# A hybrid encoder layer in float32: TensorE's four loops written out as straight code

## The chip, the cores and the metric

The kernel runs on one core of a Trainium2 chip. The metric is the device time of one launch in microseconds (us); lower is better. Of the kernel before there are three timed runs, 1295.16, 1296.4 and 1301.4 us, with the median at 1296.4 us. Beside them one execution was recorded by the hardware profiler, and every duration below comes from that one execution, whose span is 1296.8 us.

The core's engines are TensorE (PE in the profile; its weight loads are listed apart as PEld), VectorE (DVE), ScalarE (ACT), GpSimd (POOL) and SyncE (SP). Each engine has a sequencer that reads its own program, and engines meet only at semaphores. A name with a q behind it (PEldq, DVEq) is an engine's sequencer in the trace.

## What is computed

One mixer layer over 272 positions (16 learned meta tokens and 256 inputs) of width 2048, then a final norm:

```python
xn = rmsnorm(h, norm_g)
z = xn @ w_in                                   # 2048 x 16384: all branches, gates and merge gates
hy_in, hy_gate, fn_in, fn_gate, qkv, na_gate, merge = jnp.split(z, idx, axis=-1)
hy_in = short_conv(hy_in, conv_w, conv_b)
u, x1, x2 = jnp.split(hy_in, HY_ORDER + 1, axis=-1)
kf = hyena_filters(L, w1, b1, w2, b2, w3, b3, w4, freq, decay)
y_a = hyena_mixer(u, x1, x2, kf, skip) * jax.nn.silu(hy_gate)
y_b = fourier_mixer(fn_in) * jax.nn.silu(fn_gate)
y_c = neighborhood_attention(q, k, v, rpb, meta_bias) * jax.nn.silu(na_gate)
g_a, g_b, g_c = jnp.split(jax.nn.sigmoid(merge), N_BRANCH, axis=-1)
m = g_a * (y_a @ w_a) + g_b * (y_b @ w_b) + g_c * (y_c @ w_c)
return h + m @ w_out
```

## The kernel before

**Products.** Every large product is made of three float32r matmuls on high and low parts (`three`, L529 to L532: high x high, low x high, high x low). The weights are cut into slabs of 1024 x 256 elements, 1 MB each. SP streams a slab into one of four buffers `raw`; ACT rounds it into `w_hi` (L835), DVE makes `w_lo` from the rest (L1101), and PE runs 48 matmuls over it (`proj_slab`, 2 column halves x 8 k-steps x 3). `w_hi` and `w_lo` have two places each. The semaphores are `w_landed`, `hi_done`, `lo_done` and `slab_used`: SP reloads a buffer when the slab four before is split, ACT splits slab n when PE has used slab n - 2.

**Stages of PE's program.** After a small filter network and the transposition of x come four stages, each held in a hardware loop or around one:

- filters (L607): the spectra of the long convolutions, per chunk of 256 channels. The loop runs once over two chunks, two more chunks follow as straight code.
- chunks (L704): four passes `c`, one for each chunk of channels. A pass has 20 slabs (10 blocks of columns, `BLOCKS`, of two slabs each), and between the slabs the work of the three mixers on that chunk: transposes, the transforms `forward` and `inverse`, `scores`, `turn_p`, `attend`, `fnet_channels`, `fnet_tokens`. A pass ends with `fnet_tokens` (L667 and around; its last matmuls are those of L535).
- merge (L776): four passes `i` of 18 slabs each.
- output (L804): four passes of 4 slabs each.

Inside a loop the pass number is a register, so a wait such as `pe.wait_ge(proj_read, c * NBLK + (t // 2 + 1))` (L707) compares a semaphore with a register that is computed at its place.

**The other engines.** DVE, ACT and SP have loops of their own over the same passes (DVE L1283, L1389, L1407; ACT L1001, L1064, L1085; SP L349, L355, L361), and POOL loops over passes 1 to 3 of the chunks (L490). POOL's loop stores the branch results (`store_y`, L482), loads the attention bias of the next chunk as eight transfers and two more (`load_bias`, L457 and L460), adds the mask to it (L467), and then loads that chunk's first filter spectrum (`load_spectrum`, L471 and L473) into `kspec`. DVE reads `kspec` at slab t = 4 of a pass (`spectra`, L1249 to L1252), and PE waits for what DVE made of it at t = 5 (`y_full`).

**Order at the edge of a chunk pass.** The first slab of a pass is split by ACT and DVE during t = 18 of the pass before, the second during t = 19. PE's waits at t = 0 are for the evacuation of the block but one before (`proj_read`) and for the slab's low part (`lo_done`). DVE still has the last gate (L1230 to L1232) and the product with it (L1348) to do when PE comes to the edge.

Of the kernel before, what the change touches and what calls it, by code (L numbers as in the profile page):

```python
# [40 lines left out]
CH = C // CC  # L41
# [18 lines left out]
JB = D // CC  # L60
# [63 lines left out]
def build(nc, x, meta, w_stream, tables, zT, negt_in, mask_in, ident_in, params_in, mlp_in, w1, w2, w3, w4,  # L124
# [116 lines left out]
    with ExitStack() as ctx:  # L241
# [284 lines left out]
        def _(pe):  # L526
# [36 lines left out]
            def make_h4(c, j, par):  # L563

                p, n = TOK[FORDER[j]]
                if j == 0:
                    pe.wait_ge(w4_landed[par], (c - par) * 8 + 16)
                pe.wait_ge(h4_read, c * 3 + (j + 1))
                for o_ in range(2):
                    last = mm(ps[0:n, 6 + o_, :], hid[:, p:p + n], w4s[:, par, o_, :, :].rearrange("p d n -> p (d n)"),  # L570
                              start=True, stop=True)
                last.then_inc(h4_mm, 1)
# [22 lines left out]
            def filters(c, par, more):  # L595

                for j in range(3):
                    add_spectra(c, j, (0, 1, 2))
                    if j == 0:
                        make_h4(c, 2, par)  # L600
                    elif more:
                        make_h4(c + 1, j - 1, 1 - par)
                    add_spectra(c, j, (3, 4, 5))

            make_h4(0, 0, 0)
            make_h4(0, 1, 0)
            with pe.Fori(0, CH // 2 - 1) as cc:  # L607
                filters(cc * 2, 0, True)
                filters(cc * 2 + 1, 1, True)
            filters(CH - 2, 0, True)  # L610
# [11 lines left out]
            def turn(src, bank):  # L622

                for t, (p, n) in enumerate(TOK):
                    for i in range(2):
                        dst = ps[:, bank, CC * t + 128 * i:CC * t + 128 * i + 128] if t < 2 else \
                            ps[0:n, bank + 1, 128 * i:128 * i + 128]
                        last = nc.tensor.transpose(dst, src[:, i, p:p + n], ident[:, :])  # L628
                last.then_inc(t_mm, 1)
# [71 lines left out]


            pe.wait_ge(k_evac, CH * 6 + 2)
            with pe.Fori(0, CH) as c:  # L704
                for t in range(S1):
                    name, _, n = BLOCKS[t // 2]
                    if t % 2 == 0:  # L707
                        pe.wait_ge(proj_read, c * NBLK + (t // 2 + 1))
                    if t == 2:
                        pe.wait_ge(k_evac, CH * 6 + 4)  # L710
                    pe.wait_ge(lo_done, c * S1 + (NCONST + t + 1))
                    proj_slab(t % 2, 2 * (t // 2 % 2), t % 2, L - n)
                    if t == 3:
                        pe.wait_ge(proj_read, c * NBLK + 3)
                        pe.wait_ge(k_evac, CH * 6 + 6)
                        turn(u, 4)
                    if t == 4:
                        pe.wait_ge(t_lo, c * 3 + 1)
                        forward(0, 4)
                        forward(1, 5)  # L720
                    if t == 5:
                        pe.wait_ge(y_full, c * 6 + 1)
                        forward(2, 4)
                    if t == 6:
                        pe.wait_ge(proj_read, c * NBLK + 5)
                        scores(0)
                    if t == 8:
                        pe.wait_ge(p_done, c * HC + 1)
                        turn_p()
                        pe.wait_ge(proj_read, c * NBLK + 6)  # L730
                        pe.wait_ge(y_full, c * 6 + 3)
                        turn(v, 4)
                    if t == 9:
                        pe.wait_ge(pt_lo, c * HC + 1)
                        scores(1)
                        pe.wait_ge(t_lo, c * 3 + 2)
                        pe.wait_ge(ylo_done, c * 6 + 3)
                        inverse(0)
                    if t in (10, 12, 14):
                        hh = (t - 8) // 2  # L740
                        pe.wait_ge(p_done, c * HC + hh + 1)
                        attend(hh - 1)
                        turn_p()
                    if t in (11, 13):
                        hh = (t - 7) // 2
                        pe.wait_ge(o_done, c * HC + hh - 1)
                        scores(hh)
                    if t == 11:
                        pe.wait_ge(z_done, c + 1)
                        turn(x1, 4)  # L750
                    if t == 12:
                        pe.wait_ge(t_lo, c * 3 + 3)
                        forward(0, 4)
                        forward(1, 5)
                    if t == 13:
                        pe.wait_ge(y_full, c * 6 + 4)
                        forward(2, 4)
                    if t == 15:
                        pe.wait_ge(ylo_done, c * 6 + 6)
                        inverse(NM)  # L760
                        pe.wait_ge(o_done, c * HC + 3)
                        attend(3)
                    if t == 16:
                        pe.wait_ge(proj_read, c * NBLK + 10)
                        pe.wait_ge(ya_done, c + 1)
                        fnet_channels(0, 4)
                        fnet_channels(1, 5)
                    if t == 17:
                        pe.wait_ge(n1_lo, c * 3 + 1)
                        fnet_channels(2, 4)  # L770
                    if t == 19:
                        pe.wait_ge(n1_lo, c * 3 + 3)
                        fnet_tokens()


            with pe.Fori(0, JB // 2) as i:  # L776
                for t in range(S2):
                    b, part = t % 9 // 3, t % 3
                    m = t // 3
                    pair = 2 * ((2 * m + (part == 2)) % 4)  # L780
                    if part == 0:
                        pe.wait_ge(gate_done, i * 6 + (m + 1))
                        if m == 0:
                            pe.wait_ge(proj_read, NBLK * CH + 1)
                        if m == 1:
                            pe.wait_ge(yb_done, CH)
                    if part == 2:
                        pe.wait_ge(br_read, i * 6 + (m + 1))
                        if m == 0:
                            pe.wait_ge(proj_read, NBLK * CH + 2)  # L790
                        pe.wait_ge(blo_done, b + 1)
                    pe.wait_ge(lo_done, i * S2 + (NCONST + W2 + t + 1))
                    if part < 2:
                        proj_slab(t % 2, pair, part, NM)
                    else:
                        for nt in range(2):
                            for k in range(8):
                                last = three(ps[:, pair + nt, 0:NG], w_hi[:, t % 2, k, 128 * nt:128 * nt + 128],
                                             w_lo[:, t % 2, k, 128 * nt:128 * nt + 128], yb_hi[:, b, k, :], yb_lo[:, b, k, :],
                                             k == 0, k == 7)  # L800
                        last.then_inc(slab_used, 1)


            with pe.Fori(0, JB // 2) as i:  # L804
                for t in range(4):
                    half, nb = t // 2, t % 2
                    if half == 0:
                        pe.wait_ge(h_sum, i * 2 + (nb + 1))
                    if t == 0:
                        pe.wait_ge(gate_done, 3 * JB + 2)  # L810
                        pe.wait_ge(mlo_done, JB // 2)
                    if t == 1:
                        pe.wait_ge(br_read, 3 * JB + 2)
                    if t == 2:
                        pe.wait_ge(mlo_done, JB)
                    pe.wait_ge(lo_done, i * 4 + (NCONST + W3 + t + 1))
                    for tt in range(2):
                        for k in range(8):
                            kk = 8 * half + k
                            last = three(ps[:, 2 * nb + tt, 0:CC], m_hi[:, kk, 128 * tt:128 * tt + 128],  # L820
                                         m_lo[:, kk, 128 * tt:128 * tt + 128], w_hi[:, t % 2, k, :], w_lo[:, t % 2, k, :],
                                         kk == 0, kk == KT - 1)
                    last.then_inc(slab_used, 1)
# [675 lines left out]
```

## Time and profile before

| what | us |
|---|---|
| median of three timed runs | 1296.4 |
| lowest and highest of them | 1295.16, 1301.4 |
| span of the profiled execution | 1296.8 |
| PE busy in it | 1216.5 (94%) |
| DVE busy | 744.6 (57%) |
| ACT busy | 525.1 (40%) |
| POOL busy | 98.4 (8%) |

The page counts 22710 executed instructions over all engines.

Only PE is busy nearly all the time, so what matters is where PE is idle, for how long, and at which clock it works. In the profile a matmul's duration is longer than the distance to the next one's start, since matmuls overlap; distances between starts give the rate. The chunk passes begin at 123.4, 293.7, 456.4 and 618.8 us, the merge passes at 773.4, 879.7, 986.1 and 1090.8 us, the output at 1193.6 us; PE's last matmul starts at 1286.4 us.

### The profile page before, as it was taken

How to read it: one execution, taken by the hardware profiler on the slowest of the kernel's cores; microseconds unless marked ns; L12 is line 12 of the kernel's file. 1: busy time of each engine (PE TensorE's matmuls, PEld its weight loads, DVE VectorE, ACT ScalarE, POOL GpSimd, SP SyncE). 2: the span in 40 equal slices, each digit the busy share in tenths (PEclk: the TensorE clock that was granted, in tenths of full speed). 3: DMA queues.
4: the chain of work that ended last, by engine and by line, in shares of the span. 5: the costliest groups of instructions: out<-in, count | busy, mean ns of one | idle time of the engine just before them, and what ended most of it. 6: DMA issues, size and time to landing. Idle time of an engine off the chain costs nothing.

```text
span 1296.8 us, 22710 instructions
## 1 busy us (share of the span) xinstructions
PE 1216.5 (94%) x9454; PEld 1157.2 (89%) x9454; DVE 744.6 (57%) x842; ACT 525.1 (40%) x589; POOL 98.4 (8%) x130
## 2 busy tenths in 40 slices
PE   3898979989999899998999999999999999999996
PEld 1345979989999899998999999999999999999996
DVE  5675456873668736687366876544444444445454
ACT  5575334433344333443334435333333343343433
POOL 2130300022000220002200000000000000000000
PEclk9998989998999999999899999999999999999998
DMA  8144834256442564425543255454445454555652
GB/s 285 33 151 166 178 112 149 108 167 168 148 145 105 168 171 150 148 106 163 171 148 138 90 215 212 182 196 164 182 178 178 180 194 166 192 185 212 252 169 91
DMA packets 33396, 211.28 MB, mean 163 GB/s; under 512 B 4567, under 2 KB 4792, under 8 KB 10248
## 3 DMA queue, kind: packets, MB, share of 16 engines
q1 hardware_dynamic: 25976, 184.80, 40.2%
q0 software_dynamic: 7328, 25.04, 7.8%
q8 instruction: 83, 1.36, 0.4%
q14 instruction: 9, 0.07, 0.0%
HBM read 200.13 MB, written 9.70 MB: 162 GB/s over the span
## 4 chain that ended last, share of the span: by engine, by line
PE 76%; DVE 11%; issue 6%; ACT 4%; DMA 2%; POOL 1%; SPq 0%; ACTq 0%; DVEq 0%; POOLq 0%
PE ps L530 25%; PE ps L532 24%; PE ps L531 24%; ACT w_hi L835 3%; DVE gexp L1231 2%; DVE w_lo L1101 2%; PE ps L570 1%; DMA xin<-x 1%; PE ps L556 1%; DVE hm L1180 1%; DVE prod L1249 1%; DVE sd L1184 1%; DVE sd L1183 1%; DVE prod L1250 1%; PE ps L628 1%
## 5 line engine op out<-in xcount | busy, mean ns | idle before, releaser
L1101 DVE TENSOR_TENSOR w_lo<-raw,w_hi 128x2048 fp32r<-128x2048 f32 x168 | 385.5, 2295 | 426.5 <-ACT w_hi L835 426.5
L530 PE MATMUL ps<-xn_hi,w_hi 128*128 128x256 f32 (+2 forms) x2048 | 586.5, 286 | 28.9 <-issue 28.9
L531 PE MATMUL ps<-xn_lo,w_hi 128*128 128x256 f32 (+2 forms) x2048 | 584.7, 285 | 0.0
L532 PE MATMUL ps<-xn_hi,w_lo 128*128 128x256 f32 (+2 forms) x2048 | 584.5, 285 | 0.0
L835 ACT ACTIVATE w_hi<-raw 128x2048 fp32r<-128x2048 f32 x166 | 317.6, 1913 | 528.5 <-PE ps L532 528.2
L530 PEld LDWEIGHTS ps<-xn_hi,w_hi 128*128 128x128 f32 x2048 | 390.7, 191 | 31.6 <-issue 30.1
L532 PEld LDWEIGHTS ps<-xn_hi,w_lo 128*128 128x128 f32 x2048 | 390.7, 191 | 0.0
L531 PEld LDWEIGHTS ps<-xn_lo,w_hi 128*128 128x128 f32 x2048 | 389.5, 190 | 0.0
L530 PE MATMUL ps<-yb_hi,w_hi 128*128 128x256 f32 x384 | 108.8, 283 | 1.1 <-DVE yb_lo L1101 1.1
L532 PE MATMUL ps<-yb_hi,w_lo 128*128 128x256 f32 x384 | 108.6, 283 | 0.0
L531 PE MATMUL ps<-yb_lo,w_hi 128*128 128x256 f32 x384 | 108.6, 283 | 0.0
L530 PEld LDWEIGHTS ps<-yb_hi,w_hi 128*128 128x128 f32 x384 | 73.6, 192 | 1.3 <-issue 1.3
L531 PEld LDWEIGHTS ps<-yb_lo,w_hi 128*128 128x128 f32 x384 | 73.6, 192 | 0.0
L532 PEld LDWEIGHTS ps<-yb_hi,w_lo 128*128 128x128 f32 x384 | 73.6, 192 | 0.0
L530 PE MATMUL ps<-w_hi,m_hi 128*128 128x256 f32 x256 | 72.5, 283 | 0.5 <-DVE w_lo L1101 0.5
L531 PE MATMUL ps<-w_lo,m_hi 128*128 128x256 f32 x256 | 72.4, 283 | 0.0
L532 PE MATMUL ps<-w_hi,m_lo 128*128 128x256 f32 x256 | 72.4, 283 | 0.0
L990 ACT ACTIVATE y_hi<-prod 128x512 fp32r<-128x512 f32 (+1 forms) x24 | 15.2, 632 | 119.5 <-DVE prod L1252 119.5
L530 PEld LDWEIGHTS ps<-w_hi,m_hi 128*128 128x128 f32 x256 | 49.1, 192 | 0.8 <-DVE w_lo L1101 0.8
L531 PEld LDWEIGHTS ps<-w_lo,m_hi 128*128 128x128 f32 x256 | 49.1, 192 | 0.0
L532 PEld LDWEIGHTS ps<-w_hi,m_lo 128*128 128x128 f32 x256 | 49.1, 192 | 0.0
L1231 DVE RECIPROCAL gexp<-gexp 128x512 f32<-128x512 f32 x12 | 40.2, 3354 | 0.4
(239 smaller groups left out, 1304.8 us busy)
## 6 DMA issues: line engine op xcount, KB each, us to landing
raw<-w_stream SPq DMA_DIRECT2D x168, 1024.0 KB, 4.8
raw<-tables SPq DMA_DIRECT2D x4, 1024.0 KB, 20.2
kspec_grid<-kstage POOLq DMA_DIRECT2D x4, 1024.0 KB, 4.6
kspec<-kspec_grid POOLq DMA_DIRECT2D x8, 512.0 KB, 3.6
bias_t<-rpb POOLq DMA_DIRECT2D x32, 96.0 KB, 9.1
branch_y<-ystage POOLq DMA_DIRECT2D x12, 256.0 KB, 2.4
y_raw<-branch_y POOLq DMA_DIRECT2D x3, 1024.0 KB, 5.1
xin<-x SPq DMA_DIRECT2D x2, 1024.0 KB, 7.8
```

Of the source, the lines that this page charges most:

```text
L530: mm(out_ap, a_hi, b_hi, start=first, stop=False)
L531: mm(out_ap, a_hi, b_lo, start=False, stop=False)
L532: return mm(out_ap, a_lo, b_hi, start=False, stop=last)
L556: last = nc.tensor.transpose(ps[:, k % 4, p:p + n], xin[0:n, t, 128 * k:128 * k + 128], ident[0:n, 0:n])
L570: last = mm(ps[0:n, 6 + o_, :], hid[:, p:p + n], w4s[:, par, o_, :, :].rearrange("p d n -> p (d n)"), start=True, stop=True)
L628: last = nc.tensor.transpose(dst, src[:, i, p:p + n], ident[:, :])
L835: A(w_hi[:, par, :, :].rearrange("p k n -> p (k n)"), raw[:, slot, :], ACT.Copy).then_inc(hi_done, 1)
L990: ins = A(y_hi[0:n, f, :, :], prod[0:n, 2, :, :], ACT.Copy)
L1101: return V.tensor_tensor(dst, src, hi.bitcast(F32), ALU.subtract)
L1180: V.tensor_tensor(hm[0:n, :, :, :].rearrange("p o d n -> p o (d n)"), ps[0:n, 6:8, :], env.rearrange("p o d n -> p o (d n)"), ALU.mult).th ...
L1183: V.tensor_tensor(sd[0:n, 0, :, :], hm[0:n, :, 0, :], hm[0:n, :, 1, :], ALU.add)
L1231: link(V.reciprocal(gexp[:, :, :], gexp[:, :, :]))
```

## The change

Four lines: each `Fori` of PE becomes a Python loop, so PE's program has every pass written out, with constants in its waits.

```diff
-            with pe.Fori(0, CH // 2 - 1) as cc:
+            for cc in range(0, CH // 2 - 1):
                 filters(cc * 2, 0, True)
                 filters(cc * 2 + 1, 1, True)
...
-            with pe.Fori(0, CH) as c:
+            for c in range(CH):
                 for t in range(S1):
...
-            with pe.Fori(0, JB // 2) as i:
+            for i in range(JB // 2):
                 for t in range(S2):
...
-            with pe.Fori(0, JB // 2) as i:
+            for i in range(JB // 2):
                 for t in range(4):
```

The programs of DVE, ACT, POOL and SP are the same in both, loops included. PE's matmuls are the same and in the same order.

PE's program at the end of a chunk pass, before: behind the last matmuls of `fnet_tokens` stand the pass counter and the branch back to the loop's head (the head itself is shown next); `ISA` rows are waits against registers and register work.

```order
L531 MATMUL ps<-fsin_lo,y_hi 128x256
L532 MATMUL ps<-fsin_hi,y_lo 128x256
L535 MATMUL ps<-ftok_hi,y_hi 128x256
L535 MATMUL ps<-fsin_hi,y_hi 128x256
L704 REGISTER_ALU
L704 COMPARE_AND_BRANCH
L776 UNCONDITIONAL_BRANCH
```

The head of the chunk loop, before, behind the last matmul of the filters:

```order
L532 MATMUL ps<-sd_hi,filt_lo 16x512
L704 UNCONDITIONAL_BRANCH [waits k_evac]
L704 ISA
L711 ISA [waits proj_read]
L530 MATMUL ps<-xn_hi,w_hi 128x272 [waits lo_done]
```

The same place after the change, end of pass 0 and start of pass 1:

```order
L531 MATMUL ps<-fsin_lo,y_hi 128x256
L532 MATMUL ps<-fsin_hi,y_lo 128x256
L535 MATMUL ps<-ftok_hi,y_hi 128x256
L535 MATMUL ps<-fsin_hi,y_hi 128x256
L530 MATMUL ps<-xn_hi,w_hi 128x272 [waits lo_done,proj_read]
L531 MATMUL ps<-xn_lo,w_hi 128x272
```

The counter and the branch are gone, and the first matmul of the next pass follows the last of this one, with the same two semaphores waited for.

The end of a merge pass on PE, before, with what follows it when the loop is left:

```order
L530 MATMUL ps<-yb_hi,w_hi 128x256
L531 MATMUL ps<-yb_lo,w_hi 128x256
L532 MATMUL ps<-yb_hi,w_lo 128x256
L776 REGISTER_ALU
L776 COMPARE_AND_BRANCH
L804 UNCONDITIONAL_BRANCH
```

And after the change, between merge passes 0 and 1:

```order
L530 MATMUL ps<-yb_hi,w_hi 128x256
L531 MATMUL ps<-yb_lo,w_hi 128x256
L532 MATMUL ps<-yb_hi,w_lo 128x256
L530 MATMUL ps<-xn_hi,w_hi 128x256 [waits lo_done,proj_read,gate_done]
L531 MATMUL ps<-xn_lo,w_hi 128x256
```

Here too only the counter and the branch have gone from between two matmuls. PE's program has 2592 such rows before and 9333 after.

## Rows read from the trace of the kernel before

**Rows 1.** The page: busy time of PE, and its share of the span.

```profile
PE 1216.5 (94%) x9454; PEld 1157.2 (89%) x9454; DVE 744.6 (57%) x842; ACT 525.1 (40%) x589; POOL 98.4 (8%) x130
```

**Rows 2.** The page: the chain that ended last, by engine.

```profile
PE 76%; DVE 11%; issue 6%; ACT 4%; DMA 2%; POOL 1%; SPq 0%; ACTq 0%; DVEq 0%; POOLq 0%
```

**Rows 3.** Waits of PE: who waited for whom, total us, times, longest us.

```profile
PE ps L530 <- issue: 28.9, 6, 8.3
...
PE ps L530 <- DVE prod L1252: 7.7, 1, 7.7
```

**Rows 4.** Timeline of PE at pass edges: start us, us, what, [idle before].

```profile
286.05 0.28 PE L535 MATMUL ps<-fsin_hi,y_hi 80*128 80x256 f32 x1
293.68 0.59 PE L530 MATMUL ps<-xn_hi,w_hi 128*128 128x272 f32 x1 [7.34 <-issue]
...
456.42 0.59 PE L530 MATMUL ps<-xn_hi,w_hi 128*128 128x272 f32 x1 [7.66 <-issue]
...
618.83 0.59 PE L530 MATMUL ps<-xn_hi,w_hi 128*128 128x272 f32 x1 [8.30 <-issue]
...
879.65 0.58 PE L530 MATMUL ps<-xn_hi,w_hi 128*128 128x256 f32 x1 [2.00 <-issue]
```

**Rows 5.** PE's branches by loop line: ns min/median/max, first and last start.

```profile
L704 PEldq COMPARE_BRANCH  x4: 83/9381/10216, 284.2 to 771.4; - x4
...
L776 PEldq COMPARE_BRANCH  x4: 76/3654/3831, 875.5 to 1191.5; - x4
...
L804 PEldq COMPARE_BRANCH  x4: 76/215/228, 1215.4 to 1284.5; - x4
...
L607 PEldq COMPARE_BRANCH  x1: 93/93/93, 82.5 to 82.5; - x1
```

**Rows 6.** Windows, 5.6 us each: busy us (count), granted clock, DMA share, GB/s.

```profile
123.40:129.00 5.60, 5.60 (x46) 5.60 (x45) 0.00 (x0) 0.68 (x2) 1.26 (x2) 1.00 0.99 389
293.67:299.27 5.60, 5.59 (x24) 5.60 (x25) 0.00 (x0) 0.00 (x0) 0.00 (x0) 0.50 0.98 158
456.41:462.01 5.60, 5.59 (x32) 5.60 (x33) 0.00 (x0) 0.00 (x0) 0.00 (x0) 0.70 1.06 168
618.82:624.42 5.60, 5.59 (x27) 5.60 (x28) 0.00 (x0) 0.00 (x0) 0.00 (x0) 0.57 0.93 162
879.65:885.25 5.60, 5.60 (x34) 5.60 (x35) 4.27 (x4) 0.64 (x2) 0.00 (x0) 0.70 0.57 181
```

**Rows 7.** Timeline of DVE before the first pass edge: the second slab's low part.

```profile
285.00 2.29 DVE L1101 TENSOR_TENSOR w_lo<-raw,w_hi 128x2048 fp32r<-128x2048 f32 x1 [1.91 <-ACT w_hi L835]
```

**Rows 8.** The page's groups: the two steps that split a slab, busy and mean.

```profile
L1101 DVE TENSOR_TENSOR w_lo<-raw,w_hi 128x2048 fp32r<-128x2048 f32 x168 | 385.5, 2295 | 426.5 <-ACT w_hi L835 426.5
...
L835 ACT ACTIVATE w_hi<-raw 128x2048 fp32r<-128x2048 f32 x166 | 317.6, 1913 | 528.5 <-PE ps L532 528.2
```

**Rows 9.** Branches of DVE's and ACT's chunk loops, as rows 5.

```profile
L1283 DVEq COMPARE_BRANCH  x4: 50/62/68, 292.0 to 779.1; - x4
...
L1001 ACTq COMPARE_BRANCH  x4: 40/45/53, 283.2 to 770.5; - x4
```

**Rows 10.** Timeline of POOL's bias loads and masks, and of DVE's first use of kspec.

```profile
131.72 5.17 POOL L457 DMA_DIRECT2D bias_t<-rpb  x8
...
157.86 3.92 POOL L467 TENSOR_TENSOR bias_t<-bias_t,mask 128x384 f32<-128x384 f32 x4 [19.44 <-DMA bias_t<-mbias]
...
282.33 5.22 POOL L457 DMA_DIRECT2D bias_t<-rpb  x8 [0.20 <-issue]
...
303.19 5.99 POOL L467 TENSOR_TENSOR bias_t<-bias_t,mask 128x384 f32<-128x384 f32 x4 [14.11 <-DMA bias_t<-mbias]
...
168.68 0.69 DVE L1249 TENSOR_TENSOR prod<-ps,kspec 128x512 f32<-128x512 f32 x1 [10.70 <-DMA kspec<-kspec_meta]
```

**Rows 11.** A window inside chunk pass 0, columns as rows 6.

```profile
141.00:146.00 5.00, 5.00 (x44) 5.00 (x44) 3.11 (x3) 1.92 (x1) 0.00 (x0) 1.00 1.19 188
```

**Rows 12.** The page: the queue that brings instructions: packets, MB, share.

```profile
q8 instruction: 83, 1.36, 0.4%
```

## The prediction

> **What bounds the kernel now.** I read the page first. PE is busy 1216.5 of 1296.8 us [rows 1], and the chain of work that ended last runs over PE for 76% of the span [rows 2], so time comes off only where PE is idle or runs slowly. The list of waits, cut to PE, comes next. From the first chunk pass to the last matmul PE has almost only two kinds of idle time: 28.9 us in six pieces for which no engine and no transfer is named ("issue"), and one wait of 7.7 us for DVE's product with the filter spectrum [rows 3]. The timeline puts the six pieces at pass edges: 7.34, 7.66 and 8.30 us before chunk passes 1, 2 and 3, and 2.00 us before merge pass 1 [rows 4]; that leaves 28.9 - 25.3 = 3.6 us for the two edges before merge passes 2 and 3. No piece lies inside a pass, and none at an edge of the output loop.
>
> Then the sequencer's own rows, by the line of each loop. The branch that closes a chunk pass takes 9.38 us in the median and up to 10.2 us, and 0.083 us the one time it is not taken; that of the merge loop 3.65 us (0.076 us not taken); that of the output loop 0.215 us; that of the filter loop, which is never taken, 0.093 us [rows 5]. The first branch starts at 284.2 us while PE's last matmul of the pass starts at 286.05 us [rows 4, 5], so the sequencer is about two us ahead of the engine; a branch of 9.4 us leaves some 7.5 us of it to be seen, one of 3.65 us leaves about 2 us, and one of 0.2 us nothing. That is the pattern of the six pieces in size, in place and in number: three taken branches in each of two loops. The length grows with the body: 4 slabs (192 matmuls) cost nothing visible, 18 slabs 3.65 us, 20 slabs with the mixers 9.4 us. I take it that a taken branch to a far place makes the sequencer wait for code that it no longer holds.
>
> By the Trainium skill, Runtime: NRT & Kernel Launch, section Instruction fetch mechanics, code is fetched ahead sequentially and a taken branch whose target is not in the held window must fetch it from memory; the rows agree. The same section gives PE a store of 2048 instructions, and by that a merge pass (864 matmuls with 864 weight loads) would still be held and its branch would be free; the row of 3.65 us speaks against it, and the row decides. By the page the merge edges would give nothing.
>
> **The change, part by part.** It removes PE's branches and register arithmetic and moves nothing else.
>
> *Chunk edges.* The idle time is 7.34 + 7.66 + 8.30 = 23.3 us [rows 4]. To it belongs what the clock loses: after such a gap the granted clock is 0.50, which is the lower level of 1.2 GHz, for some microseconds. In 5.6 us from the restart PE starts 24, 32 and 27 matmuls where an undisturbed pass starts 46 [rows 6]. That is 22 + 14 + 19 = 55 matmuls too few, at 5.6 / 46 = 0.122 us each, 6.7 us. Sum 30.0 us.
>
> *Merge edges.* 2.00 + 3.6 = 5.6 us of idle time [rows 3, 4]. After the first the clock fell too (34 matmuls in place of 46: 12 x 0.122 = 1.5 us [rows 6]); I count nothing for the other two. Sum 7.1 us.
>
> *The model of the ends.* Idle time is counted from a matmul's modelled end, 0.28 us after its start, while an undisturbed successor starts 0.12 us after it. So each of the six edges hides 0.16 us more: 1.0 us.
>
> *Output and filter loops.* The output branch of 0.215 us leaves no idle time at PE, and the filter branch is not taken: 0 us, covered by the sequencer's lead of two us. If that cover were gone it would be 3 x 0.2 = 0.6 us. The register arithmetic before the waits is covered the same way.
>
> *What is late next.* A gain at an edge stands only if everything that pass needs early is there 10 us sooner. The first slab's low part was made before the edge, and the second's at 285.00 + 2.29 = 287.3 us [rows 7]; PE will want it one slab (48 x 0.122 = 5.9 us) after 286.2 us, at 292.1 us. Later slabs need ACT's 1.91 us and DVE's 2.29 us one after the other [rows 8], 4.2 us in a rhythm of 5.9 us. ACT and DVE keep their loops, and I looked there for the same stall, hidden so far under PE's: their branches take 0.045 and 0.062 us in the median, 0.068 us at most [rows 9]. So nothing of that sort waits to come out. What remains is POOL's chain, the second rival below.
>
> *Fetching the straight code.* The instructions do not become more for the chip to read: 1.36 MB came through the instruction queue for 22710 executed instructions [rows 12], 60 bytes for each, so the long bodies are read anew in each pass already. The question is whether reading ahead keeps up when the transfer engines are full. In pass 0 they were (share 1.19 at 141 to 146 us) and PE stayed busy for all of the 5.00 us at full clock [rows 11]. I take 0 us; the bounds are 0 and, if one read per edge were exposed as it is today, 10.2 us each.
>
> Sum: 30.0 + 7.1 + 1.0 = 38.1 us. From the profiled execution's 1296.8 us that gives 1258.7 us. The median of the runs is 0.4 us under the profiled span, so 1258.3 us for a median.
>
> **Rivals.**
>
> *The spectrum comes late (POOL's chain).* In pass 0 this happened: masks began at 157.86 us, 34.5 us after the pass began, and DVE waited 10.7 us for `kspec` [rows 10], PE 7.7 us [rows 3]. In pass 1 the masks begin at 303.19 us. Against a pass that will start at 286.2 us that is 17.0 us in, 17.5 us sooner than in pass 0. They take 2.1 us longer (5.99 against 3.92 us), and 7.7 us are needed, so 7.7 us are to spare. But without PE's pause the slab transfers run on beside the bias transfers, as in pass 0, where 26.1 us went by from the first bias transfer to the masks against 20.9 us here [rows 10]. With those 5.2 us, 2.5 us are to spare. It decides if the bias needs more than some 28 us. Its price: a wait of 2 us and a slow restart of 2 us at three passes, 12 us, hence 1270 us; at its worst three times the 7.7 + 2.7 us of pass 0, 31 us, hence 1289 us. Chance 0.14.
>
> *Reading ahead falls behind.* The branch took 9.4 us where the transfer engines were full (0.98 to 1.06 just behind those edges) and 3.65 us at 0.57 [rows 5, 6], so a read of code under load is slow. If one read stalls PE at each of the three chunk edges for half of what it costs today, 15 us come back: 1273 us. Rows 11 speak against. Chance 0.07.
>
> *The branch is not the cause.* Then the change does not do what it is for. The chain shows DVE in 11% [rows 2], and PE's restart comes soon after DVE's last gate of the pass. For it: that nearness. Against: at the merge edges DVE is idle and PE pauses still, and the branch's own length fits each time. It would give 1296 us. By the Trainium skill, Advanced Engine Details and Errata, section Control Flow Timing, a compare-and-branch is about 108 ns; by that figure alone six branches are worth 0.65 us, and the time would be this rival's. The trace has that price only for branches not taken and for short bodies. Chance 0.03.
>
> *Slower: every new stretch of code costs.* PE now enters all its code once and never comes back to held code. One packet of the instruction queue is 1.36 MB / 83 = 16.4 KB [rows 12], so PE's program is some 75 packets. If entering one cost an exposed 3.65 us as the merge branch does, 270 us would be added: 1530 us. It beats the gain from 38.1 / 75 = 0.5 us a packet. Against it: inside the passes, which span many packets, PE has no unexplained idle time [rows 3]. Chance 0.02. Another 0.02 goes to a clock that PE loses for want of its pauses (3% over the last 1160 us would eat the gain).
>
> **How the numbers follow.** The forecast, all edges gone and nothing in their place, has 0.72: 1258.3 us, with 1254 to 1263 us for its own errors (the counts in the windows, two slow restarts left out, and the runs' own scatter). The rivals have 0.14, 0.07, 0.03 and 0.04. The range leaves out the slower cases and half of the two partial ones: 1253 to 1273 us. A difference of 0.5% (6.5 us) is about what the measurement tells from none. Faster by more: 0.72 + 0.14 + 0.07, and a little off for extreme forms, 0.92. Within 0.5%: 0.04. Slower: 0.04.
>
> **What would show it.** In the profile after: no idle time named "issue" at PE behind 123 us; chunk passes 1 to 3 lasting 152 to 153 us from start to start, where passes 1 and 2 last 162 us now; merge passes about 103 us in place of 105 to 106; granted clock 1.00 right behind each edge; PE's last matmul at about 1248 us, and about 10 us of tail as now. The second rival would show as waits of L530 for DVE's product L1252 in passes 1 to 3, the third as "issue" inside passes. A kernel above 1290 us would make the reading of the branch rows wrong.

## The result

The changed kernel takes 1259.88 us in the median of four runs (1259.82 to 1260.72). Against the kernel before, timed on the same chip (1296.2 us), the ratio is 0.9718, with a 95% interval of 0.9689 to 0.9748. The forecast was 1258.3 us in a range of 1253 to 1273 us. The profiled execution has a span of 1258.3 us, where 1258.7 us was worked out.

The page of the changed kernel, first its busy times (answering to [rows 1]), then the granted clock in 40 slices and the instruction queue (to [rows 12]):

```profile
PE 1206.9 (96%) x9454; PEld 1148.0 (91%) x9454; DVE 745.4 (59%) x842; ACT 524.7 (42%) x589; POOL 98.1 (8%) x130
...
PEclk9998989999999999999999999999999999999999
...
q8 instruction: 74, 1.21, 0.4%
```

PE does the same 9454 matmuls. It is busy 9.6 us less, since fewer of them run at the lower clock, and the span is 38.5 us less. The waits of PE, as [rows 3], have no line of L530 for "issue" any more:

```profile
PE ps L546 <- ACT hid L855: 10.6, 2, 5.8
PE ps L530 <- DVE sd_lo L1101: 7.2, 5, 2.9
PE ps L530 <- DVE prod L1252: 6.4, 1, 6.4
...
PE ps L530 <- DVE w_lo L1101: 1.3, 3, 0.6
```

The timeline of PE at the edges before chunk pass 1 and merge pass 1, as [rows 4]: the first matmul of a pass starts 0.12 us after the last of the pass before, and no idle time stands behind the lines:

```profile
283.26 0.28 PE L535 MATMUL ps<-fsin_hi,y_hi 80*128 80x256 f32 x1
283.38 0.29 PE L530 MATMUL ps<-xn_hi,w_hi 128*128 128x272 f32 x1
...
846.68 0.28 PE L532 MATMUL ps<-yb_hi,w_lo 128*128 128x256 f32 x1
846.80 0.28 PE L530 MATMUL ps<-xn_hi,w_hi 128*128 128x256 f32 x1
```

And 5.6 us from each of the three chunk edges on, the columns as in [rows 6] (PE busy and its count, PEld, DVE, ACT, POOL, granted clock, share of the transfer engines, GB/s):

```profile
283.38:288.98 5.60, 5.60 (x47) 5.60 (x46) 5.53 (x4) 0.00 (x0) 2.88 (x5) 1.00 0.95 250
436.70:442.30 5.60, 5.60 (x47) 5.60 (x46) 5.53 (x4) 0.00 (x0) 2.86 (x5) 1.00 1.01 262
590.17:595.77 5.60, 5.60 (x47) 5.60 (x46) 5.51 (x4) 0.00 (x0) 4.48 (x7) 1.00 0.89 251
```

Where PE started 24, 32 and 27 matmuls it now starts 47, at full clock, with the transfer engines just as full as before. Chunk passes 1 to 3 last 153.3, 153.5 and 152.6 us from start to start, merge passes 1 and 2 last 102.7 us each. By stage, the four chunk passes together went from 650.0 to 620.7 us (29.3 us less) and the four merge passes from 420.15 to 412.21 us (7.9 us less). The first chunk pass began at 122.05 us and not at 123.4 us, 1.35 us that no loop of the change explains: with the filter loop kept it began at 122.2 and 121.7 us in two of the kernels below.

### The profile page after: what moved, and what is told of

It reads as the page before. It is cut to its first block, busy times and chain, and to the rows that moved or that the text cites. A ratio compares the mean times of both kernels' runs of the same rounds, so it can differ in the third digit from the quotient of the medians.

```text
span 1258.3 us, 22460 instructions
## 1 busy us (share of the span) xinstructions
PE 1206.9 (96%) x9454; PEld 1148.0 (91%) x9454; DVE 745.4 (59%) x842; ACT 524.7 (42%) x589; POOL 98.1 (8%) x130
## 4 chain that ended last, share of the span: by engine, by line
PE 67%; DVE 12%; issue 10%; ACT 5%; DMA 3%; POOL 2%; ACTq 0%; SPq 0%; DVEq 0%; POOLq 0%
PE ps L530 22%; PE ps L532 21%; PE ps L531 21%; ACT w_hi L835 3%; DVE w_lo L1101 2%; DVE gexp L1231 2%; DMA kspec<-kspec_meta 1%; PE ps L570 1%; DVE prod L1250 1%; DVE prod L1249 1%; PE ps L556 1%; DVE hm L1180 1%; POOL bias_t L457 1%; DMA xin<-x 1%; DVE sd L1183 1%
## 5 line engine op out<-in xcount | busy, mean ns | idle before, releaser
L530 PE MATMUL ps<-xn_hi,w_hi 128*128 128x256 f32 (+2 forms) x2048 | 582.5, 284 | 0.7 <-DVE w_lo L1101 0.7
L530 PEld LDWEIGHTS ps<-xn_hi,w_hi 128*128 128x128 f32 x2048 | 387.0, 189 | 2.7 <-issue 1.6
L530 PE MATMUL ps<-yb_hi,w_hi 128*128 128x256 f32 x384 | 108.7, 283 | 1.1 <-DVE yb_lo L1101 1.1
L530 PEld LDWEIGHTS ps<-yb_hi,w_hi 128*128 128x128 f32 x384 | 73.6, 192 | 1.3 <-issue 1.3
L530 PE MATMUL ps<-w_hi,m_hi 128*128 128x256 f32 x256 | 72.5, 283 | 0.6 <-DVE w_lo L1101 0.6
L530 PEld LDWEIGHTS ps<-w_hi,m_hi 128*128 128x128 f32 x256 | 49.1, 192 | 0.8 <-issue 0.8
```

What stands on the lines that cost most here:

```text
L530: mm(out_ap, a_hi, b_hi, start=first, stop=False)
```

## The experiments

The kernel before was timed beside each set of experiments; its median was 1295.51 us beside the first four, 1296.08 us beside the next four and 1294.33 us beside the last four.

### One loop at a time

Each takes a part of the change: the chunk loop alone (one line, shown here), the merge loop alone (one line), and the output and filter loops alone (two lines).

```diff
-            with pe.Fori(0, CH) as c:
+            for c in range(CH):
```

> Only the chunk loop is straight code; filters, merge and output loops stay. If the six taken branches are the cause and add up, this takes 30 us and half of the 1.0 us for the modelled ends: 1296.2 - 30.5 = 1265.7 us, no idle time named issue at the chunk edges, and about 2 us of it at each of the three merge edges, with a branch of 3.5 to 3.8 us on the merge loop's line. If the branch is not the cause (the last gate of DVE is), the time stays at 1296 us.

> Only the merge loop is straight code. By the branches: 5.6 us of idle time, 1.5 us of slow restart and 0.5 us of ends go, 1296.2 - 7.6 = 1288.6 us; the chunk edges keep 7.3 to 8.3 us each. By the page figure of a 2048-instruction store the merge branch would never have cost anything and the time would be 1296 us.

> Only the filter and the output loops are straight code. My theory: no change, 1296.2 us within 1 us, because the filter branch is not taken and the output branch of 0.2 us lies under the sequencer's lead. Rival: any branch costs its visible part, 0.6 us less. Rival, slower: code that was held in the output loop must now be read, and an exposed read of 3.65 us for each of some 4 more packets would give 1310 us.

Measured: chunks alone 1265.82 us (ratio 0.9774, interval 0.9738 to 0.981); merge alone 1284.38 us (0.991, 0.9879 to 0.9942); output and filters alone 1294.81 us (1.000, 0.9981 to 1.002). In microseconds these are 29.7, 11.1 and 0.7 less than the kernel before. The three sum to 41.5 us against 36.3 us for all together; with intervals of 3 to 5 us on each they agree.

The chunk loop's part came as expected. The merge loop's median gain is 3.5 us more than the 7.6 us asked for, which is at the edge of its interval (7.5 to 15.7 us). By the traces the merge stage itself took 412.2 us with this loop straight, where it took 420.15 us before: 7.9 us. The rest lies elsewhere, and the profile shows where some of it does. The waits of PE and the branch row with the merge loop straight (chunk edges kept):

```profile
PE ps L530 <- issue: 20.9, 3, 7.3
...
L704 PEldq COMPARE_BRANCH  x4: 83/8661/9256, 281.2 to 765.7; - x4
```

The three chunk edges were shorter in this execution than in the one profiled before (20.9 us against 23.3 us), which is taken for scatter: PE meets the edited loop only behind the last of these edges. Output and filters alone change nothing that can be measured, as the row of 0.215 us in [rows 5] said. The rival by which the chunk edges wait for DVE's last gate falls: in the first kernel DVE's program is unchanged, and PE's three idle times at the chunk edges are gone; the three at the merge edges stayed:

```profile
PE ps L530 <- issue: 5.1, 3, 2.0
...
L776 PEldq COMPARE_BRANCH  x4: 79/3376/3877, 844.5 to 1158.4; - x4
```

The packets of the instruction queue tell how much code is read. In the changed kernel 9454 matmuls and 9454 weight loads came in 74 packets, some 256 instructions each (an estimate: the few rows of registers and waits are left out). The packets are 83 before; 76 with the chunks straight, 77 with the merge straight, 88 with output and filters straight:

```profile
q8 instruction: 76, 1.25, 0.4%
```

```profile
q8 instruction: 77, 1.26, 0.4%
```

```profile
q8 instruction: 88, 1.44, 0.4%
```

So three taken branches of the chunk or the merge loop cost 7 or 6 packets, two or more for each. The traces show them where they belong: a merge pass before has 9 packets (876.6 to 982.9 us, and the same in the next pass), one of the changed kernel 6 or 7; a chunk pass had 12 and has 9 or 10. That these are packets read ahead and thrown away is a reading of the count. The output loop is the other way round: straight code needs 5 packets more, since its loop was not read again (3 repeats of some 394 instructions are 4.6 packets of 256).

### How long the branch is, and what makes it so

Two chunk passes in one body, so that one branch is taken and not three:

```diff
-            for c in range(CH):
+            with pe.Fori(0, CH // 2) as cc:
+                for c in (cc * 2, cc * 2 + 1):
```

> As the changed kernel (merge, output and filters straight), but the chunk passes stand in a loop of two iterations with two passes each: one taken branch in place of none. If the cost is per taken branch whatever the length of the body, 1259.9 + 10 = 1270 us, with one branch of 9 to 10 us on the loop's line and one idle time of 7 to 8 us before pass 2 and none before passes 1 and 3. If the branch's length grows with the body (it went from 3.65 us at 18 slabs to 9.4 us at 20 slabs with the mixers), it is longer than 10.2 us and the time is above 1272 us.

Measured: 1267.28 us (0.9782, 0.975 to 0.9813), 7.4 us above the changed kernel. The branch and the wait:

```profile
PE ps L530 <- issue: 7.5, 1, 7.5
...
L704 PEldq COMPARE_BRANCH  x2: 83/4682/9282, 432.4 to 747.4; - x2
```

The time is nearer to the 1270 us of one cost per taken branch than to a longer branch. The taken one has 9.28 us, the same as with half the body: between these two bodies, both out of reach, the length does not grow. It does change with what else is moved, as the next two show. First POOL issues the ten bias transfers of the next pass ahead of its wait for branch 2, all loops kept:

```diff
                 store_y(c - 1, 0, ya_done)
-                store_y(c - 1, 2, yc_done)
                 pool.wait_ge(smax_done, c * HC)
-                load_bias(c)
+                issue_bias(c)                   # the ten transfers of load_bias
+                store_y(c - 1, 2, yc_done)
+                finish_bias(c)                  # the wait for them, and the masks
```

> The kernel before, all loops kept; only POOL issues the ten bias transfers of the next pass some 19 us earlier (right behind store_y of branch 0, before it waits for branch 2), so that they are mostly done at the chunk edge. If the 9.4 us of the chunk branch against 3.65 us of the merge branch is queueing behind those transfers, the chunk branch falls to between 3.5 and 5 us, the idle time at each chunk edge to 2 to 3 us with a shorter slow restart, and the time by some 18 us, to 1278 us. If the length comes from the distance of the jump or the size of the body, it stays at 9.4 us and the time at 1295.5 us.

Measured: 1292.52 us (0.9979, 0.996 to 0.9998), 3.6 us less, not 18. The three branches (the loop's line is L708 here) and the transfer engines over the same stretches:

```profile
L708 PEldq COMPARE_BRANCH  x1: 8914/8914/8914, 281.1 to 281.1; - x1
...
L708 PEldq COMPARE_BRANCH  x1: 6837/6837/6837, 443.2 to 443.2; - x1
...
L708 PEldq COMPARE_BRANCH  x1: 7107/7107/7107, 603.4 to 603.4; - x1
```

```profile
281.00:290.00 9.00, 2.33 (x20) 2.12 (x18) 6.67 (x4) 1.44 (x2) 4.22 (x5) 0.76 0.78 297
443.00:450.00 7.00, 2.40 (x21) 2.19 (x19) 5.90 (x3) 1.51 (x2) 3.61 (x4) 0.96 0.91 344
603.00:611.00 8.00, 2.81 (x23) 2.61 (x22) 6.68 (x4) 1.66 (x2) 2.06 (x3) 0.93 0.88 288
```

The edge was not empty: the slabs that the bias had held up were moved there now (297 to 344 GB/s, 191 to 217 GB/s in the kernel before). So the move changed the kind of the load and took little of it away. The next kernel leaves the bias transfers of passes 1 to 3 out, and with them the right bias:

```diff
-                load_bias(c)
+                masks_only(c)                   # L467 alone, no transfer
```

> The kernel before, all loops kept, but POOL moves no bias in passes 1 to 3: the eight transfers of 96 KB and the two of 32 KB are left out, the masks are added to what pass 0 left (so the attention scores of passes 1 to 3 use the wrong bias). Moving those transfers 19 us ahead shortened the chunk branch from 9.3, 9.5 and 10.2 us to 8.9, 6.8 and 7.1 us, while the transfer engines stayed 0.78 to 0.91 busy at the edge with slabs that the bias had held up. If queueing behind other transfers is all that separates the chunk branch from the merge branch, it falls to 3.4 to 5 us here, the idle times to 1.7 to 3 us, and the time to about 1275 us. If the chunk edge has something of its own (a body of 2480 matmuls and weight loads against 1728), the branch stays above 6.5 us and the time above 1288 us.

Measured: 1284.11 us (0.9921, 0.9899 to 0.9942), 10.2 us less. The branch rows (lines L711 and L783 here) and the wait:

```profile
L711 PEldq COMPARE_BRANCH  x4: 83/5658/5943, 279.8 to 754.7; - x4
...
L783 PEldq COMPARE_BRANCH  x4: 76/3630/3707, 858.7 to 1176.1; - x4
...
PE ps L537 <- issue: 17.0, 6, 4.0
```

Neither expectation holds in full. The chunk branch falls from 9.4 to between 5.6 and 5.9 us, so some 3.6 us of it go with the bias transfers (over the three branches the transfer engines are 0.61 to 0.64 busy now, 0.90 to 1.00 before). But 2 us above the merge branch stay.

The packet records of the instruction queue show where in the branch the time lies. In the kernel before, the packet comes 6.5, 6.8 and 7.4 us after a chunk branch began (the first branch began at 284.2 us, and there is no packet of this queue until 290.6 us), and the branch ends 2.7 to 2.8 us behind its packet's start. At the merge edges the packet comes after 1.2, 1.1 and 1.0 us, and the branch ends 2.6 to 2.7 us behind it. Without the bias transfers it comes after 3.3 to 3.6 us at the chunk edges, and the branch ends 2.3 us behind it. So the packet itself and what follows it cost nearly the same at all these edges (2.3 to 2.8 us), and the difference between chunk and merge edges, the 2 us that stay included, is time before the packet starts. That fits a queue of other transfers ahead of it. Slab transfers still run there; that they alone are the 2 us was not shown, and neither was a part of the chunk loop's own.

### How far back a branch may go for nothing

The output loop with two passes in a body, all else straight:

```diff
-            for i in range(JB // 2):
+            with pe.Fori(0, JB // 4) as ii:
+                for i in (ii * 2, ii * 2 + 1):
```

> As the changed kernel, but the output passes stand in a loop of two iterations with two passes each: 384 matmuls with 384 weight loads a body, one taken branch. Before, a body of half that length had branches of 0.215 us and no idle time. If the code that can be returned to is shorter than 768 instructions, this branch takes about 3.6 us as the merge branch did and PE idles 2 us at the edge, where none of the kernels so far had an idle time; two more packets come through the instruction queue than the length of the code asks for. If it is 2048 instructions, the branch stays near 0.2 us and nothing is seen.

The branch's row, and the instruction queue from the page:

```profile
L804 PEldq COMPARE_BRANCH  x2: 76/156/235, 1201.1 to 1247.2; - x2
```

```profile
q8 instruction: 71, 1.16, 0.4%
```

Measured: the taken branch has 0.235 us, PE has no idle time at the edge, and three packets fewer come than for straight code. A body of 768 is held. A single run gave 1261.07 us. Then, in the changed kernel, the merge loop was put back and shortened by leaving out a part of the low x high products, to 1368 and 1584 matmuls and weight loads (shown for the slabs of the projection; the others are shortened alike):

```diff
-                        proj_slab(t % 2, pair, part, NM)
+                                if 8 * nt + k < 6:          # 12 in the second kernel
+                                    last = three(...)
+                                else:
+                                    last = two(...)
```

> The changed kernel with the merge loop put back, and part of its third products (low x high) left out, so that a body has 684 matmuls and 684 weight loads, 1368, beside 26 rows of registers and waits. It is the length that is asked for: a body of 768 had a branch of 0.235 us, one of 1728 had 3.65 us. If code is held for 2048 instructions and some 512 of them are always read ahead (six taken branches cost 13 packets of 256 instructions beyond the code's own length, two each), a body under 1536 can be returned to: branch 0.2 us, no idle time at the merge edges, and fewer packets than straight code would need. If the limit lies between 768 and 1368, the branch is 3 to 4 us.

> As the one before with fewer products left out: 792 matmuls and 792 weight loads, 1584. With 2048 held of which 512 are read ahead this is too long: branch 3.3 to 3.9 us, idle time of 1.5 to 2 us at the merge edges, two packets more for each of the three taken branches. If 2048 instructions can be returned to in full, it is 0.2 us here, but then the body of 1728 would have been free as well. Rival: a limit between 1584 and 1728, branch 0.2 us.

The branch and the instruction queue with the body of 1368, then the same two with that of 1584:

```profile
L780 PEldq COMPARE_BRANCH  x4: 76/210/240, 827.2 to 1083.6; - x4
```

```profile
q8 instruction: 52, 0.85, 0.3%
```

```profile
L780 PEldq COMPARE_BRANCH  x4: 76/210/235, 837.0 to 1121.9; - x4
```

```profile
q8 instruction: 53, 0.87, 0.3%
```

The shorter body behaves as expected. The longer one misses: it too is free, and the rival expectation is the one that came true. The trace has 34 rows of registers, waits and branch in each merge pass, and not 26. So a body of 1584 + 34 = 1618 costs 0.21 us a branch in the median, and the merge body before, 1728 + 34 = 1762, 3.65 us. The packets agree: from 74, three repeats of 1618 instructions that are not read again (19.0 packets) and four passes shorter by 144 (2.25) give 53. The trace shows it directly: between 830 and 1128 us, over three of the four merge passes, only two queues have packets, and the instruction queue q8 is not among them. These are the two over 830 to 1122 us:

```profile
q1 hardware_dynamic: 8020, 58.49, 58.7%
q14 instruction: 2, 0.02, 0.0%
```

ACT, DVE and SP work on in this stretch, so I read q8 as the queue of PE's code. A single run of each gave 1190.53 and 1228.85 us, with work left out, so that these times are not comparable with the others.

By the Trainium skill, Runtime: NRT & Kernel Launch, section Instruction fetch mechanics, PE's store holds 2048 instructions and is filled in blocks of 256; by the same section a taken branch stalls when its target is outside a window of two blocks. The runs agree with neither as a limit for a loop: a body of 1762 is under 2048 and stalls, and bodies of 768 to 1584 matmuls and weight loads are over 512 and do not. One block always read ahead would leave 1792, two would leave 1536 (estimates from the page's figures), and neither lies between 1618 and 1762, so neither is the limit by subtraction alone. Where in a block a loop begins may decide it. No run moved the merge loop by a few instructions, so the limit is shown for this program's layout only.

### POOL's chain

In the changed kernel the spectrum of passes 1 to 3 came late for DVE. DVE's first use in pass 1, and POOL's masks ahead of it, as [rows 10]:

```profile
319.95 0.69 DVE L1249 TENSOR_TENSOR prod<-ps,kspec 128x512 f32<-128x512 f32 x1 [2.00 <-DMA kspec<-kspec_meta]
```

```profile
279.53 5.21 POOL L457 DMA_DIRECT2D bias_t<-rpb  x8 [0.20 <-issue]
284.68 1.58 POOL L460 DMA_DIRECT2D bias_t<-mbias  x2
306.61 5.98 POOL L467 TENSOR_TENSOR bias_t<-bias_t,mask 128x384 f32<-128x384 f32 x4 [20.35 <-DMA bias_t<-mbias]
```

DVE waited 2.00, 2.14 and 1.29 us in the three passes, and PE did not wait for its product there. The same move of the bias as above, now on the changed kernel:

> The changed kernel with the same move of the bias transfers. In the changed kernel DVE waited 2.0, 2.1 and 1.3 us for kspec in passes 1 to 3, and PE did not. With the move those three waits go (kspec lands some 15 us earlier), and the time stays: 1259.9 us within 1 us. Rival: the waits of DVE cost PE something that the trace does not name, or store_y of branch 2, now behind the bias transfers, holds up DVE at t = 19: 1 to 6 us either way.

Measured: 1258.11 us (against before 0.9715, 0.9676 to 0.9755), 1.8 us under the changed kernel; of DVE's four waits for the spectrum only that of pass 0 is left (7.6 us in the list of waits, once). Against the kernel before, the two ratios (0.9715 and 0.9718) are the same, so that is the expected nothing, or a little. And the two loads of pass 0 exchanged:

```diff
-            load_bias(0)
             load_spectrum(0, 0)
+            load_bias(0)
```

> The changed kernel with two lines of POOL exchanged: the first spectrum is loaded before the bias of pass 0, not behind it. In pass 0 PE waits 6.4 us for DVE's product and restarts slowly (2.7 us at the most). If the spectrum is what it waits for, both go: 1259.9 - 9 = 1251 us. Rival: the bias, 5 us later then, becomes late for the first scores at t = 6, and the gain is under 4 us.

Measured: 1255.78 us in the median, four runs of 1249.29, 1255.73, 1255.83 and 1259.07 us (against before 0.9703, 0.9661 to 0.9744). In the profiled run, the fastest, PE has no wait for DVE's product at all. The 4 us by which its median is under the changed kernel's are less than the 9 us asked for, and its interval holds the changed kernel's ratio. The runs spread over 10 us, so in other executions something takes a part back, and no profile shows what; DVE waited 7.4 us in three places for later spectra even in the fastest. Both moves together:

> The changed kernel with both moves of POOL: the first spectrum ahead of the first bias, and the bias of the next pass issued ahead of the edge. The first alone gave 1255.8 us in the median with runs from 1249.3 to 1259.1, the second alone 1258.1 us. If the profile of the first is typical (span 1247.7 us, no wait of PE for DVE's product in pass 0), both together give 1249 to 1252 us. If the wait in pass 0 comes back in some runs for another reason, the median stays near 1255 us.

Measured: 1250.37 us in the median of six runs (1246.67 to 1252.03), as expected, against before 0.9659 (0.9629 to 0.9689); the span of its profile, taken of the fastest run, is 1245.1 us, with the clock at 9 in 39 of the 40 slices and no wait for a spectrum left:

```profile
PEclk9999999999999999999999999999999999999998
```

Its median is the lowest of all kernels that leave no work out. It is 9.5 us under the changed kernel's; taken by the ratios, each to the kernel before beside it, the difference is 0.6%, or 7.6 us. The two intervals just touch at 0.9689, so that it is faster is likely, and its size is uncertain.

## Why the prediction was right

**Chunk edges, 30.0 us.** The kernel with this loop alone gives 29.7 us, and the chunk stage of the changed kernel is 29.3 us shorter, where 30.5 us were summed with its half of the modelled ends. Both halves are seen: 23.3 us of idle time gone, and 47 matmuls in 5.6 us where 24 to 32 were.

**Merge edges, 7.1 us.** Alone 11.1 us by the medians, with 7.5 us at the low end of the interval. The merge stage is 7.9 us shorter, both there and in the changed kernel, where 7.6 us were summed with the ends.

**The sum against the span.** Profile against profile, 38.5 us went where 38.1 us were summed. That this is so close is in part luck: the two stages gave 37.3 us, and 1.35 us came before the first chunk pass, where the change takes no branch away.

**Output and filter loops, 0 us.** Alone 0.7 us, with an interval on both sides of 0.

**What is late next.** ACT's and DVE's loops had nothing hidden, as [rows 9] said. POOL's chain was the tight place: 26.1 us from the first bias transfer to the masks were expected and 27.1, 27.6 and 26.6 us measured, with 28 us named as the point where it costs. It stayed under it. DVE waited 1.3 to 2.1 us for the spectrum, and PE did not wait for DVE's product in these passes. With only the chunks straight PE waited for that product twice, once for 6.4 us and once for 0.4 us. So the rival did not happen, but there was little to spare.

**Reading ahead.** No read of straight code was exposed, with the transfer engines at 0.89 to 1.01. One sentence was wrong: that the chip would read as much as before. It reads 9 packets fewer (74 against 83). The single loops account for 8 of them: 13 that went with the branches of the chunk and merge loops, less 5 that the output loop had saved. The 60 bytes for each instruction were no support either: they divide the packets of PE's queue by the instructions of all engines.

**From span to median.** The forecast is 1.6 us low: 38.1 us were taken from the median, and the medians are 36.3 us apart, while the two profiled executions are 38.5 us apart. The term that seems too large for a median run is the first one, the idle time at the chunk edges: 23.3 us in the execution that I read, 20.9 us with the merge straight, and 21.7 us with output and filters straight, all with the same chunk loop. That fits the profiled execution's own time: a run is timed 1.5 us above its span (1259.83 us and 1258.3 us for the changed kernel), so an execution with a span of 1296.8 us is one of some 1298.3 us, 1.9 us above the median, and not 0.4 us as I had it by comparing a span with a timed median.

**The reading of the branch.** That a taken branch to code no longer held stalls the sequencer is shown, by leaving the branches out, by making bodies short enough, and by the packets: each long branch before, and in the kernel without bias transfers, ends 1.3 to 1.6 us behind the end of one. My note that its length grows with the body was wrong: it is a step, at a body between 1618 and 1762. Above it the length changes with how long the packet takes to start: bias transfers make 3.6 us of the chunk branch, and for 2 us more the cause stays open.

## What to carry to other kernels

Look at the sequencer's own rows: a closing branch of several us, with as much idle time as it exceeds the sequencer's lead, was here code being read again. Write out, or shorten until the branch takes 0.2 us, only the loops of the engine that has these rows; loops of short bodies, and those of engines that wait anyway, may stay. When a pause on the critical engine goes, every chain that used to finish inside the pause (here POOL's bias and spectrum) has lost that much slack, and it is worth moving it forward in the same step.

## What the runs showed beyond this

In this kernel a loop body of 1618 instructions on TensorE is repeated for 0.21 us and without reading it again; one of 1762 costs 3.65 us and two packets of 16 KB more for each turn, with the transfer engines 0.42 to 0.47 busy. The branch of the chunk loop (2480 matmuls and weight loads), with the engines 0.90 to 1.00 busy, costs 9 to 10 us, and 5.6 to 5.9 us with the bias transfers gone; the difference is time before the packet with the code starts. Writing out the output loop, which is held, cost 5 packets and gained nothing that can be measured.
